# A two-layer trunk with delta rule, attention, convolution and memory on one core: slices of the convolution between replies, value products laid by tokens, and openings that run two weight chunks together

## The reference

```python
for layer in range(2):
    h = rms_norm(x, norm_pre[layer])
    y = ab_mixer(h, ...) if layer == 0 else conv_mixer(h, ...)
    x = x + rms_norm(y, norm_post[layer])
    h = rms_norm(x, xattn_norm_pre[layer])
    m = rms_norm(mem, mem_norm[layer])
    x = x + rms_norm(memory_cross_attention(h, m, ...), xattn_norm_post[layer])
```

## Time and profile before

| | us |
|---|---|
| median of 3 executions | 2610.19 (2605.46 to 2610.9) |
| the profiled execution | 2604.95 |
| its span, first to last instruction | 2603.2 |
| PE busy | 2475.8 |
| DVE busy | 1315.7 |
| ACT busy | 808.6 |
| POOL busy | 299.5 |

### The profile page before, as it was taken

How to read it: one execution, slowest core, us unless ns; L and a number is a source line. 1 busy time by engine, 2 the same in 40 slices (tenths; PEclk the granted TensorE clock), 3 DMA queues, 4 the chain that set the end, 5 groups by cost and what they waited for, 6 DMA issues and landing times.

```text
span 2603.2 us, 30751 instructions
## 1 busy us (share of the span) xinstructions
PE 2475.8 (95%) x12244; PEld 2055.0 (79%) x12244; DVE 1315.7 (51%) x1689; ACT 808.6 (31%) x1348; POOL 299.5 (12%) x198
## 2 busy tenths in 40 slices
PE   7999998999999999989989989999999999999986
PEld 6788787878887777978877778888888888887765
DVE  5555545554355656763355575333433343433746
ACT  4232322223244345542233441122212222322442
POOL 3010110202011011001121140000000000010304
PEclk9999999999999999999999989999999999999997
DMA  9522322156355332443321222323232322332212
GB/s 173 88 57 49 66 50 68 45 56 65 51 129 90 65 89 65 154 161 130 96 84 63 76 81 92 101 75 116 91 100 78 114 92 92 98 98 96 73 50 80
DMA packets 222976, 227.76 MB, mean 87 GB/s; under 512 B 9360, under 2 KB 216464, under 8 KB 222864
## 3 DMA queue, kind: packets, MB, share of 16 engines
q1 hardware_dynamic: 222720, 225.64, 34.5%
q10 hardware_dynamic: 144, 0.52, 0.1%
HBM read 221.94 MB, written 4.19 MB: 87 GB/s over the span
## 4 chain that ended last, share of the span: by engine, by line
PE 64%; issue 24%; DVE 5%; POOL 3%; ACT 1%; DMA 1%; SPq 1%; POOLq 0%; ACTq 0%; DVEq 0%
PE acc L797 20%; PE acc L799 19%; PE acc L798 19%; POOL work L1782 2%; DVE weights_lo L1145 1%; DMA weights_raw<-in_ab_w_in 1%; DVE work L1548 1%; PE m L941 1%; PE m L1086 1%; PE m L1098 1%; POOL small L1759 0%; ACT work L719 0%; PE m L1021 0%; DVE input_lo L1561 0%; PE m L776 0%
## 5 line engine op out<-in xcount | busy, mean ns | idle before, releaser
L797 PE MATMUL acc<-input_hi,weights_hi 128*128 128x512 f32 (+1 forms) x3168 | 1242.6, 392 | 53.0 <-DVE weights_lo L1145 22.4
L799 PE MATMUL acc<-input_hi,weights_lo 128*128 128x512 f32 (+1 forms) x3168 | 1214.8, 383 | 1.8 <-issue 1.8
L798 PE MATMUL acc<-input_lo,weights_hi 128*128 128x512 f32 (+1 forms) x3168 | 1213.1, 383 | 0.0
L797 PEld LDWEIGHTS acc<-input_hi,weights_hi 128*128 128x128 f32 x3168 | 601.3, 190 | 188.8 <-issue 35.7
L1145 DVE TENSOR_TENSOR weights_lo<-weights_raw,weights_hi 128x1024 fp32r<-128x1024 f32 x400 | 534.8, 1351 | 374.2 <-ACT weights_hi L409 373.0
L799 PEld LDWEIGHTS acc<-input_hi,weights_lo 128*128 128x128 f32 x3168 | 600.4, 190 | 117.2
L798 PEld LDWEIGHTS acc<-input_lo,weights_hi 128*128 128x128 f32 x3168 | 601.9, 190 | 109.5 <-issue 1.9
L409 ACT ACTIVATE weights_hi<-weights_raw 128x1024 fp32r<-128x1024 f32 x400 | 418.5, 1057 | 617.9 <-PE acc L799 576.9
L1821 POOL TENSOR_TENSOR work<-work 128x512 f32<-128x512 f32 x56 | 72.6, 1296 | 429.0 <-ACT work L671 425.0
L1759 POOL TENSOR_TENSOR small<-small 128x4 f32<-128x4 f32 (+1 forms) x20 | 25.5, 1275 | 741.7 <-DVE small L1329 382.8
L1527 DVE COPY work<-acc 128x512 f32<-128x512 f32 x64 | 41.6, 686 | 134.8 <-PE acc L799 121.6
(11 more groups left out here) (240 smaller groups left out, 1864.9 us busy)
## 6 DMA issues: line engine op xcount, KB each, us to landing
weights_raw<-in_ab_w_in SPq DMA_DIRECT2D x128, 512.0 KB, 5.3
weights_raw<-in_c_w_in SPq DMA_DIRECT2D x128, 512.0 KB, 3.7
weights_raw<-in_m_w_kv SPq DMA_DIRECT2D x32, 512.0 KB, 3.4
weights_raw<-in_ab_w_out SPq DMA_DIRECT2D x32, 512.0 KB, 4.5
weights_raw<-in_m_w_q SPq DMA_DIRECT2D x32, 512.0 KB, 3.3
weights_raw<-in_c_w_out SPq DMA_DIRECT2D x32, 512.0 KB, 3.9
residual<-in_x SPq DMA_DIRECT2D x32, 256.0 KB, 5.2
weights_raw<-in_m_w_o SPq DMA_DIRECT2D x16, 512.0 KB, 3.3
```

Of the source, the lines that this page charges most:

```text
L797: pe.matmul(out, w_hi[:, o:o + P], hi(kt), start=kt == 0, stop=False)
L798: pe.matmul(out, w_hi[:, o:o + P], lo(kt), start=False, stop=False)
L799: last = pe.matmul(out, w_lo[:, o:o + P], hi(kt), start=False, stop=kt == last_kt)
```

## The change

- `D_SLOTS` ends three slots earlier (60 for 63). The "r" and "s" of every token chunk get slots of their own, and between "y4" and "p5" one quarter is left where there were two.
- POOL's mask products alternate between `c_t` and `gam`, and each waits for a step one earlier: the one for "p1" for "qk" (L1253), which is the last reader of `gam`, no longer for "y0" (L1257).
- DVE convolves in slices: one per quarter of a chunk, behind that quarter's reply; the gates (L1356) and ACT's tanh move accordingly.
- Value chunks of the memory are multiplied with the tokens as the stationary operand, so that the result has the layout that was reached by transposes. ACT scales it out of PSUM (`take_values`); the transposes, their DVE scaling and copying go.
- In the three openings PE takes two chunks together, tile by tile of x, first the eight products with x's high half, then the four with its low half. Five splits are put between the norm's tiles, two neighbours together, and the wide sum of squares moves from chunk 5 to 7 of DVE's list, behind the split of chunk 8.

```diff
-D_SLOTS, B_SLOTS = weighted(D_HOPS, 12, 63, D_REPLY), weighted(B_HOPS, 18, 63, B_REPLY)
+D_SLOTS, B_SLOTS = weighted(D_HOPS, 12, 60, D_REPLY), weighted(B_HOPS, 18, 63, B_REPLY)
-ACT_AHEAD, VECTOR_AHEAD = (1, 4, 6, 9, 11, 13), (3, 6, 8, 11, 13, 15)
+ACT_AHEAD, VECTOR_AHEAD = (1, 6, 7, 11, 12), (5, 8, 9, 13, 14)
+        level = lambda s: (c_t, gam)[s % 2]
...
+            def take_values(q):
+                l, j, pair = q // 4, q % 4, P_KV + q
+                act.wait_ge(chunk_used, done_at(pair))
+                act.wait_ge(acc_free, 2 * pair)
+                act.wait_ge(*MG("pow"))
+                for m in range(2):
+                    v0 = (l * 2 + m) * MH * HD + 256 * (j - 2)
+                    act.activation(mv[:, v0:v0 + 256], bank(pair, m, 256), ACT.Copy, scale=t2[:, m:m + 1])\
+                        .then_inc(acc_free, 1)
             for c in range(32):
                 split(C_KV + c + 1)
+                if c in (12, 16, 28):
+                    take_values(c // 4 - 1)
...
-            def value_transposes(l, j, pair):
...
+            def value_chunk(g, pair, kt0, l, between):
...
+                    for m in range(2):
+                        out = bank(pair, m, 256)
+                        tok = slice(m * P, (m + 1) * P)
+                        pe.matmul(out, mem_h(H_hi, l, kt)[:, tok], w_hi[:, w], start=kt == 0, stop=False)
+                        pe.matmul(out, mem_h(H_hi, l, kt)[:, tok], w_lo[:, w], start=False, stop=False)
+                        last = pe.matmul(out, mem_h(H_lo, l, kt)[:, tok], w_hi[:, w], start=False, stop=kt == KT - 1)
...
+            def opening(r, c0, p0):
+                high = lambda kt: NA(f"hi{kt}", r) if kt > 1 else NV(f"hi{kt}", r)
+                pe.wait_ge(acc_free, 2 * p0)
+                for q in range(4):
+                    pe.wait_ge(lo_ready, c0 + 2 * q + 2)
+                    for k in range(4):
+                        kt = 4 * q + k
+                        x = slice(kt * T, (kt + 1) * T)
+                        at_ = lambda n, j: ((c0 + 2 * q + n) % SPLIT_SLOTS) * CW + k * 256 + j * P
+                        pe.wait_ge(*high(kt))
+                        for n, j in ((0, 0), (0, 1), (1, 0), (1, 1)):
+                            o = at_(n, j)
+                            pe.matmul(bank(p0 + n, j), w_hi[:, o:o + P], H_hi[:, x], start=kt == 0, stop=False)
+                            pe.matmul(bank(p0 + n, j), w_lo[:, o:o + P], H_hi[:, x], start=False, stop=False)
+                        pe.wait_ge(*NV(f"lo{kt}", r))
+                        for n, j in ((0, 0), (0, 1), (1, 0), (1, 1)):
+                            o = at_(n, j)
+                            last = pe.matmul(bank(p0 + n, j), w_hi[:, o:o + P], H_lo[:, x], start=False,
+                                             stop=kt == KT - 1)
+                            if k == 3 and j == 1:
+                                last.then_inc(chunk_used, 1)
...
-            def convolve(it, sec, n):
+            def convolve(it, sec, n, k):
...
+                if k == 0:
+                    dve.wait_ge(chunk_used, ab_done(pair))
+                    if n:
+                        dve.wait_ge(*EV.last())
+                    TTO(conv_in, bank(1 + sec, n), rs[:, :], ALU.mult).then_inc(acc_free, 1)
+                    dve.wait_ge(acc_free, 2 * pair + n + 1)
+                    TS(dst, conv_in, tap(3), None, ALU.mult).then_inc(*EV.did())
+                else:
                     dve.wait_ge(*EV.last())
-                    STT(out=dst[:, d:T], in0=conv_in[:, 0:T - d], scalar=tap(3 - d), in1=dst[:, d:T],
-                        op0=ALU.mult, op1=ALU.add).then_inc(*EV.did(f"c{sec}{n}" if d == 3 else None))
+                    STT(out=dst[:, k:T], in0=conv_in[:, 0:T - k], scalar=tap(3 - k), in1=dst[:, k:T],
+                        op0=ALU.mult, op1=ALU.add).then_inc(*EV.did(f"c{sec}{n}" if k == 3 else None))
...
-                for w in {5: (8,), 8: (4, 2, 1)}.get(c, ()):
+                for w in {7: (8,), 8: (4, 2, 1)}.get(c, ()):
...
-                    pool.wait_ge(*(GV("nt", i) if s == 0 else GV("y0", i) if s == 1 else GM(f"p{s - 1}", i)))
-                    pool.tensor_tensor(tiles(c_t), tiles(n_t), over_tiles(level_mask(s), 8), ALU.mult)\
+                    pool.wait_ge(*(GV(("nt", "qk", "y0")[s], i) if s < 3 else GM(f"p{s - 2}", i)))
+                    pool.tensor_tensor(tiles(level(s)), tiles(n_t), over_tiles(level_mask(s), 8), ALU.mult)\
```

116 lines of the change are left out of this document (55 added, 61 removed).

## The result

The changed kernel takes 2573.23 us (median of four executions, 2572.85 to 2575.26), the kernel before beside it 2609.07 (2605.46 to 2610.9): a ratio of 0.9866, with a 95% interval of 0.9849 to 0.9883. The forecast was 2590 with a range of 2577 to 2603. By the two traces, 31.6 of them are in the span (2603.2 to 2571.6); the rest is that the profiled execution of before (2604.95) is one of its quickest, while that of after (2573.36) lies at its median.

What follows compares the result with a forecast made beforehand. PE's list was taken to bound the kernel (busy 2475.8 of 2603.2). 2604.95 - 18.0 (rounds) - 5.7 (values) - 13.2 + 14.4 (openings) + 5 (clock) = 2587.4; -17.5 put on 2607.8 gave 2590, range 2577 to 2603.

Steps and rivals of the forecast that it cites:

- What goes in the rounds: Delta rounds: PE's waits for POOL's mask (7.0) and before "s" (14.4) go, 24.3 us with the overlap of 18 waits.
- What comes in the rounds: Delta rounds: a new wait of 1.3 a round before "p5", 5.3 in all, and 1.0 before "r0".
- The 1.0 before "r0": Delta rounds: "r0" stands behind the split of chunk 11, 0.25 a round, 1.0 in all (0 to 2).
- The other distances between hops stay as they were: Delta rounds: the prediction's statement that nothing else changes between steps; no term was put on it.
- Memory values: Memory value chunks: transposes and PE's waits before them go, products run as fast; a gain of 5.7 (2 to 8).
- Openings, what goes: Three openings: earlier start, two later waits gone, less clock loss; a gain of 4.4 each, 13.2 in all.
- Openings, what comes: Three openings: new waits before chunk 8 and for the sums, 4.8 an opening, 14.4 in all.
- A: Each opening: PE waits before chunk 8 for its split, which stands behind DVE's copies of pair 0; 2.3.
- B: Each opening: PE waits for the sums in the middle of chunk 9; 2.5.
- the terms for the clock: Openings: 5 lost in all (0 to 10) by clock falls at six new waits; 0.7 gained at each opening's start.
- Rival 1: Openings cost less: no clock fall at the six waits and waits shorter by 1; 2579 us, chance 0.14.
- The median: Whole kernel: the change of -17.5 was put on 2607.8, between 2605.46 and 2610.19, giving 2590.

Runs made afterwards that it cites:

- one_mask: The changed kernel with one mask buffer, as before, POOL writing each mask behind the step "y" that read it: 2595.13 us.
- whole_conv: The changed kernel with DVE's four convolution operations in a row and the tanh steps where they stood before: 2591.95 us.
- hop_late: The changed kernel with the delta round's last step, "ft", back on quarter 63 instead of 60: 2581.87 us.
- old_values: The changed kernel with the transposed memory values of the kernel before: 2582.30 us.
- split_first: The changed kernel with only the split of chunk 8 put ahead of the copies of pair 0 in the openings: 2574.48 us.
- opening_order: The changed kernel with DVE's openings reordered: splits of chunks 8 and 9, copies of pair 0, all four sums, pair 1's copies at chunk 10: 2564.05 us.
- slots_only: The kernel before with the delta steps on quarters 12 to 60 instead of 12 to 63, one mask buffer and whole convolutions kept: 2617.86 us.
- hop_early: The kernel before with "ft" alone moved from quarter 63 to 60: 2627.97 us.

## Why the prediction was wrong

**What goes in the rounds.** Right. The waits for the mask (7.0) and before "s" (14.4) are gone. Undone by themselves they cost 17.8 (one_mask, falls of the clock included) and 14.8 (whole_conv) in the delta rounds of the trace, with the new steps. The overlap of 0.16 a wait holds: by the waits of before and after in the rounds, 28.3 (with 5.8 of "issue" and 1.1 for weights in the fourth round) less 5.0 is 23.3; with 18 waits fewer at 0.16 it is 26.2, and up to the first product of the memory 26.5 were won, from the first "tr" on.

**What comes in the rounds.** "p5" waits 4.5, and 5.1 with the overlap, where 5.3 were worked out from start to start. The 1.0 before "r0" did not come.

**The failed step.** "The other distances between hops stay as they were" is where the prediction went wrong. It counts only from hop to hop and leaves out the distance from the last one, "ft", to the end of the round, and so puts the back-edge at nothing without a reason. That distance grew by three quarters, and with it the gaps at two back-edges shrank from 5.8 us to 0.48; hop_late brings back 4.2 as gaps and 5.4 in all, a fall of the clock included. (Between hops, too, "s3" to "r4" and "s4" to "r5" shrank to one quarter, at no cost that the trace shows.) The rows stood in the view from which the earlier trace rows was taken, between the two that were used, and were passed over since nothing was named as their cause. A row of idle PE time must be put on the account even so, with 0 and its whole size as bounds: taken whole it would have brought 2584, with a low end of 2571.

**Memory values.** 5.7 forecast; 5.6 between the memory's norm and the first norm of x, and 5.7 when undone. The stretch scatters by 1.5 with the clock (279.2 or 280.7 with the new code, 284.9 or 286.4 with the old), so a term of some tenths cannot be read from it. But the value products run no slower with x as stationary operand: in the median one starts 0.120 after the one before (384 products, L1010 to L1012 in after), as the products of the keys and those of old_values do.

**Openings, what goes.** The start waits 2.18 in place of 2.96 (0.8; forecast 0.9), and the two later waits are gone. Right.

**Openings, what comes.** A, the wait before chunk 8, was 2.1 (forecast 2.3). B, the wait for the sums, was 0.79 where 2.5 was forecast, although split_first shows 2.3 to 2.4 for it once A is down to 1.0. Its size had been worked out as if PE ran at full clock from chunk 8 on (8.2 for 36 products), and the loss of clock behind A was then added as a term of its own. But from chunk 8 to the sums PE took 10.06 (1359.13 to 1369.98 less 0.79), 1.9 more than the 8.2: the slow stretch had used up most of the lateness of the sums. The clock fell three times and not six. What an opening brings and costs is thus even, -0.5 for all three by the table of stages, where +6.2 was forecast (-13.2, +14.4 and +5). Of the 6.7 between them B is 5.1, three times 1.7; the rest lies in the terms for the clock. This is the second step that failed. Rival 1 came nearest, for a reason that it did not name.

**The median.** The change was put on 2607.8, the middle of the four times. The five medians of before lie between 2609.1 and 2610.4, so 2 us were lost there.

**In numbers.** 17.5 were forecast. The rounds brought 8.5 more: 5.8 at the edges (gaps of 5.8 less the 0.48 left, and 0.5 of overlap), 1.3 at a wait for weights with its overlap, 1.0 and 0.2 at the new waits, and 0.2 that is left over. The openings brought 6.7 more, the start 1.8 by chance. Off go 2.3 by the fall of the clock at the memory's norm, 0.1 at the values and 0.4 at the end. That makes 31.7, and the spans differ by 31.6.

**On POOL and DVE.** The early mask ran from 308.11 to 310.49 with no more than its 2.38, and DVE's L1308, which reads two inputs from SBUF, is drawn from 310.35 with its usual 1.23: an overlap of 0.14 in the records.

```profile
310.35 1.23 DVE L1308 TENSOR_TENSOR work<-constants,work 128x1024 f32<-128x1024 f32 x1
```

```profile
308.11 2.38 POOL L1830 TENSOR_TENSOR work<-work,constants 128x1024 f32<-128x1024 f32 x1 [4.14 <-DVE work L1304]
```

The Trainium skill (SBUF — State Buffer, "Who interferes with whom") has an exclusive lock here, which would allow no such overlap. The records of DVE alone overlap as well: L1307, just before, ends at 310.43, 0.08 behind the start of L1308. So L1308 started as soon as L1307 let it, and 0.14 is too close to what the records do anyway to speak for or against the lock. PE waits nowhere near it, and it priced nothing.

## What to carry to other kernels

Put every idle row of the bounding engine on the account, those without a cause too, and when a table of positions is squeezed ask of each step what the distance to the end of the loop's body does, not only the distance to the step before. Two waits in a row on one engine are no sum: work out the second with the first, and its loss of clock, in place; then test the order that removes both at once, since removing one alone may show nothing (split_first) and removing both 9 us (opening_order). Where an engine stands at a loop's edge and no releaser is named, look at the transfers of instructions too. A change of step positions, a buffer and a slicing may each be worth nothing or less alone (slots_only, hop_early); undo them one at a time from the finished kernel as well as doing one alone.
